# A hybrid decoder block: feature projections by seven products instead of eight, with weight parts streamed from DRAM

## The chip, the cores and the metric

One core of one Trainium2 chip runs the whole program. The metric is the device time in microseconds, the median of three runs. TensorE does the matrix products, VectorE (DVE), ScalarE (ACT) and GpSimd (POOL) the rest; SyncE (SP) issues transfers.

## What is computed

`x` has 4096 positions of 1024 features in f32. The layer is

```python
h = RMSNorm(x)
q, k, v, gk_lr, gate_g, u_p, gate_p, q_m, gate_m = split(h @ w_in)
gk = log_sigmoid(gk_lr @ w_gk_up + b_gk) / 16
o_gla = RMSNorm(gated_linear_attention(q, k, v, gk)) * silu(gate_g)  # 4 heads, chunks of 64
o_pool = (causal means of u_p - u_p) @ pool_w * pool_scale * silu(gate_p)
o_mem  = softmax(q_m @ k_m^T / 8) @ v_m * silu(gate_m)  # k_m, v_m from RMSNorm(mem)
y = RMSNorm(x + concat(o_gla, o_pool, o_mem) @ w_out)
```

`w_in` has 2576 columns: q and k 256 each, v 512, a low rank part of 16, gates 512 + 256 + 256, u_p 256 and q_m 256.

## The kernel before, in words

The sequence goes in 16 blocks of 256 positions. `run_blocks` writes block 0 (`first`), block 1 (`second`), a loop over blocks 2 to 14, block 15 (`last`) and a tail; every engine has its own list of instructions, ordered by hand, and semaphores between them.

**Precision.** A factor of a product stands in SBUF as two f16 parts, high and low, each weight group scaled by a power of two; a product is three matmuls (high x high, high x low, low x high) added up in PSUM. That is `split` (L371 to 378).

**Projections.** The block of x, transposed, 8 tiles of 128 features by 256 positions, is normalised in place (`normalise`, L1052) and split into `xn`: ACT makes the high parts (L725), GpSimd the low ones (L1416, two instructions of 1024 columns). The weights' parts are in `whl`, resident. `features` (L380) makes 256 output features of a block in one bank: 2 column halves x 8 tiles x 3 = 48 matmuls of 256 columns. A loop block has eight such groups (q, k, four of gates, u, qm), and the values in two halves (`split` with x as the weights, 24 matmuls of 512 columns each). The order on TensorE: low rank part (L425), q, logits of the decay (L440), k, a sum over partitions for the scale of the mixed block (`mix_sum`, L402), values, first two gates, u, qm, last two gates. ACT or DVE read each bank once: q and k on DVE with the decays (L1169 to L1179), the others on ACT (L843 values, L854 gates with silu, L869 u, L878 qm).

**Attention and output.** Then come the transposes of the keys (L512), the scores in chunks (L522), memory scores (L539), states, transposes of the softmax's probabilities (L563), the attention's products (L571, L577, L647) and the sums of squares of the heads (L585). The four quarters of the output projection of the block before (`out_proj`, L388, 24 matmuls of 512 columns each) stand between these steps. They need the mixed block's two parts: ACT's high part (`mixed_hi`, L787, after the values' first copy) and DVE's low part (`mixed_lo`, L1076 to L1093, whose first four small steps make the scale from bank 6). ACT turns the key transposes over (L902), after which it loads a table (L905) for the exponentials; output rows are squared and normalised on ACT (`norm_y`, L793 to L798). ACT's copy of the low rank part is L804.

**Preparation.** In block 0 each weight group gets a total (sums of squares on ACT, a matmul `total` on TensorE), a scale (`weights_scale`, DVE), high parts (`weights_hi`, ACT L733, ten pieces of 2048 columns) and low parts (`weights_lo`, DVE L1031, ten too); the memory's keys and values are multiplied out in f32 (L343, L348). W_out is read twice from DRAM in 8 tiles: squares in block 0, parts (`out_hi` L774, `out_lo` L1034) in block 1, resident in `wo`.

**Queues.** SP issues all transfers in one order: inputs, the next x block, W_out's tiles, and per block twice a residual in and, once its row is normalised (L1104 adds the residual), a store.

## Time and profile before

| | us |
|---|---|
| median of 3 runs | 1498.22 (1496.93 to 1498.28) |
| the profiled execution | 1497.08 |
| its span | 1495.6 |
| mean granted TensorE clock | 0.988 |
| busy: TensorE, VectorE, ACT, GpSimd | 1436.3, 709.6, 637.4, 215.1 |
| bytes moved by DMA | 73.70 MB |

The span runs from the first to the last instruction. The low rank matmuls (L425) mark a block's start: 22.9 for block 0, 136.35 for block 1, 226.78 for block 2, and from there one every 87.8 us until 1368.39, block 15. In the trace's rows an operation shows its start, its length, engine, line, operation, output and input tiles, the matmul's weight shape (128*128) and its moving shape. Groups show busy us, mean ns of one, and idle time ahead with what ended it. Times are of one execution.

### The profile page before, as it was taken

The numbers are of one execution on the slowest core, as the hardware profiler recorded it, in microseconds if no ns is written. First come the engines' busy times: TensorE is split into PE (matmuls) and PEld (weight loads), VectorE is DVE, ScalarE is ACT, GpSimd is POOL, SyncE is SP. The second block draws the span as 40 slices with busy tenths as digits, with TensorE's granted clock in tenths as the row PEclk, the third lists the DMA queues.
The fourth block names the chain that finished last, engine by engine and source line by source line (L and its number), as shares of the span: only waits on it lengthen the run. The fifth ranks groups of instructions, "written<-read, shape, count | busy, mean of one in ns | idle before, by whom it ended". The sixth has DMA issues, their size and how long they took to land.

```text
span 1495.6 us, 28176 instructions
## 1 busy us (share of the span) xinstructions
PE 1436.3 (96%) x11766; PEld 1043.1 (70%) x11766; DVE 709.6 (47%) x1357; ACT 637.4 (43%) x1135; POOL 215.1 (14%) x204
## 2 busy tenths in 40 slices
PE   4958999999999999999999999999999999999996
PEld 3747767768676776867667686776768677676852
DVE  4565454371635436172543717255271635527152
ACT  6676353442525344252533425254342624434241
POOL 2021020211201021020112102011210201121000
PEclk9979999999999999999999999999999999999998
DMA  9321201020110102001010200101020010201001
GB/s 361 127 85 60 83 29 58 1 85 0 40 44 28 56 0 84 0 28 56 20 64 0 84 0 28 56 14 70 0 84 0 28 56 4 80 0 57 1 29 71
DMA packets 18560, 73.70 MB, mean 49 GB/s; under 512 B 2016, under 2 KB 4320, under 8 KB 15712
## 3 DMA queue, kind: packets, MB, share of 16 engines
q1 hardware_dynamic: 18096, 72.96, 13.2%
q8 instruction: 24, 0.39, 0.1%
q10 hardware_dynamic: 432, 0.28, 0.1%
q14 instruction: 8, 0.07, 0.0%
HBM read 56.46 MB, written 16.78 MB: 49 GB/s over the span
## 4 chain that ended last, share of the span: by engine, by line
PE 93%; ACT 2%; DVE 2%; DMA 1%; issue 1%; POOL 1%; DVEq 0%; ACTq 0%
PE bank L377 77%; PE bank L539 2%; PE bank L563 2%; PE bank L571 2%; PE bank L577 2%; PE bank L585 2%; PE bank L647 1%; PE bank L550 1%; PE bank L440 1%; PE bank L425 1%; ACT whl L733 1%; PE bank L522 1%; PE bank L324 1%; PE bank L343 0%; PE bank L348 0%
## 5 line engine op out<-in xcount | busy, mean ns | idle before, releaser
L377 PE MATMUL bank<-arena,whl 128*128 128x256 f16 x6144 | 684.2, 274 | 0.0
L377 PEld LDWEIGHTS bank<-arena,whl 128*128 128x128 f16 x6144 | 602.0, 98 | 80.8 <-issue 4.0
L377 PE MATMUL bank<-arena 128*128 128x512 f16 x1536 | 344.0, 381 | 6.4 <-DVE arena L1093 6.4
L377 PEld LDWEIGHTS bank<-arena 128*128 128x128 f16 x1536 | 147.7, 98 | 181.3 <-issue 15.4
L1228 DVE SCALAR_TENSOR_TENSOR arena<-arena 64x256 f32<-64x256 f32 x60 | 25.2, 420 | 306.1 <-POOL arena L1440 304.7
L377 PE MATMUL bank<-whl,arena 128*128 128x512 f16 x768 | 168.5, 379 | 0.0
L854 ACT ACTIVATE arena<-bank,sca 128x512 f32<-128x512 f32 x60 | 41.3, 688 | 242.1 <-PE bank L377 242.1
L377 PEld LDWEIGHTS bank<-whl,arena 128*128 128x128 f16 x768 | 75.3, 99 | 86.8
L1416 POOL TENSOR_TENSOR arena<-arena 128x1024 f16<-128x1024 f32 x32 | 76.1, 2398 | 310.5 <-ACT arena L725 310.5
L1433 POOL TENSOR_TENSOR arena<-arena 128x542 f32<-128x542 f32 x16 | 17.4, 1090 | 657.4 <-ACT arena L869 657.4
L1267 DVE TENSOR_REDUCE mx<-bank 128x2 f32<-128x512 f32 x64 | 41.2, 684 | 141.6 <-PE bank L539 141.6
L1408 POOL TENSOR_TENSOR arena<-arena 128x1024 f32<-128x1024 f32 (+2 forms) x45 | 69.2, 1538 | 222.4 <-ACT arena L708 220.0
L1279 DVE SCALAR_TENSOR_TENSOR arena<-arena,rsum 128x256 f16<-128x256 f32 x128 | 61.6, 533 | 57.2 <-ACT arena L936 57.2
L1104 DVE SCALAR_TENSOR_TENSOR arena<-bank,sca,arena 128x512 f32<-128x512 f32 x64 | 47.8, 749 | 66.5 <-DMA arena<-in_x 42.4
L926 ACT ACTIVATE arena<-bank,nm,sca 128x256 f32<-128x256 f32 x128 | 71.2, 560 | 3.9 <-ACT nm L916 2.2
L936 ACT ACTIVATE arena<-arena,rsum 128x256 f16<-128x256 f32 x128 | 56.0, 499 | 25.6 <-DVE rsum L1273 25.6
L1093 DVE SCALAR_TENSOR_TENSOR arena<-arena,sca 128x2048 f16<-128x2048 f32 x16 | 37.6, 2352 | 49.8 <-ACT arena L787 49.8
L843 ACT ACTIVATE arena<-bank,sca 128x512 f32<-128x512 f32 x32 | 21.8, 685 | 88.6 <-PE bank L377 88.6
L793 ACT ACTIVATE arena<-arena 128x1024 bf16<-128x1024 f32 x32 | 33.6, 1050 | 55.6 <-DVE arena L1104 55.6
L1307 DVE COPY arena<-bank 128x1024 f16<-128x1024 f16 x64 | 43.9, 688 | 17.9 <-PE bank L563 17.9
L1052 DVE SCALAR_TENSOR_TENSOR arena<-arena,sca 128x256 f32<-128x256 f32 x128 | 51.9, 477 | 0.0
L878 ACT ACTIVATE arena<-bank 64x512 f16<-64x512 f32 x32 | 18.9, 592 | 69.8 <-PE bank L377 69.3
(164 smaller groups left out, 1441.1 us busy)
## 6 DMA issues: line engine op xcount, KB each, us to landing
arena<-in_xt SPq DMA_DIRECT2D x16, 1024.0 KB, 5.1
arena<-in_x SPq DMA_DIRECT2D x32, 512.0 KB, 3.3
out<-arena SPq DMA_DIRECT2D x32, 512.0 KB, 2.6
stage<-in_w_out SPq DMA_DIRECT2D x16, 512.0 KB, 4.8
arena<-in_w_v SPq DMA_DIRECT2D x1, 2048.0 KB, 14.6
whl<-in_w_mem SPq DMA_DIRECT2D x1, 2048.0 KB, 16.8
arena<-in_w_g SPq DMA_DIRECT2D x1, 2048.0 KB, 17.0
arena<-in_w_p SPq DMA_DIRECT2D x1, 2048.0 KB, 7.8
```

Of the source, the lines that this page charges most:

```text
L377: mm = nc.tensor.matmul(ap, lhs, rhs, start=k == 0 and n == 0, stop=(k, n) == last)
L854: nc.scalar.activation(gate[:, g:g + 2, :], bank[b][:, :].rearrange("p (a t) -> p a t", a=2), ACT.Silu, scale=sc_in[:, w:w + 1]).then_inc( ...
L926: a = nc.scalar.activation(pr[n % 2][:, h, :], bank[2 + n % 2][:, h * 256:(h + 1) * 256], ACT.Exp, bias=nm[:, 2 * n + h:2 * n + h + 1], sc ...
L936: a = nc.scalar.activation(phl[n % 2][:, 0, h, :], pr[n % 2][:, h, :], ACT.Copy, scale=rsum[:, 2 * n + h:2 * n + h + 1])
L1052: a = nc.vector.scalar_tensor_tensor(xb[:, k, :], xb[:, k, :], gx[:, k:k + 1], sq[:, 1, :], ALU.mult, ALU.mult)
L1093: nc.vector.scalar_tensor_tensor(mhl[:, 1, :, :], mixed, s_m, mhl[:, 0, :, :], ALU.mult, ALU.subtract).then_inc(m_lo, 1)
L1104: nc.vector.scalar_tensor_tensor(yb[:, c], bank[h][:, :], sc_out, yb[:, c], ALU.mult, ALU.add).then_inc(y_add, 1)
L1267: nc.vector.tensor_reduce(mx[:, 2 * n:2 * n + 2], bank[2 + n % 2][:, :].rearrange("p (h m) -> p h m", h=2), AX.X, ALU.max).then_inc(max_ok, 1)
L1279: a = nc.vector.scalar_tensor_tensor(phl[n % 2][:, 1, h, :], pr[n % 2][:, h, :], rsum[:, 2 * n + h:2 * n + h + 1], phl[n % 2][:, 0, h, :], ...
L1307: nc.vector.tensor_copy((pt0 if first else pt)[:, p, :, t * P:(t + 1) * P], b16[b].rearrange("p (a b) -> p a b", b=P)).then_inc(pt_out, 1)
L1408: nc.gpsimd.tensor_tensor(sq[:, 0:half, :], sq[:, 0:half, :], sq[:, half:2 * half, :], ALU.add).then_inc(sq_add, 1)
L1416: nc.gpsimd.tensor_tensor(xn[:, 1, k, :], xb[:, k, :], xn[:, 0, k, :], ALU.subtract).then_inc(x_lo, 1)
```

## The change

Two blocks of 256 features are projected together, by Strassen's scheme in Winograd's form. With two halves of the output features, two of the input features and two of the positions, the 8 block products become 7. The groups are QK (q and k), UM (u and qm), GG (the gates of the linear attention) and PM (pool and memory gates). A product is 2 x 4 x 3 = 24 matmuls of 128 columns. The 7 of a group come in three phases of 3, 3 and 1 (`PHASES`), into two banks that each hold two regions; between phases ACT copies regions to SBUF (`early_copies`, `second_copy`, `third_copy`) and the next phase goes on accumulating in the same regions; DVE adds copy and region for each quarter of the result (`add_11`, `add_12`, `add_2`). Phases of two groups alternate.

The x side needs four more inputs, B11-B12, B12+B22, that minus B11, and B21 minus that (`SG3`, `SG1`, `SG2`, `SG4`): GpSimd makes them and all low parts, ACT the high parts. The weight side needs four combinations too, made once in block 0 (on DVE for QK, on GpSimd for the others), so each group has 7 pieces of 1024 columns, each with a high and a low part. QK's, UM's and the values' parts are resident. GG's and PM's parts are written to DRAM in block 0 and W_out's in block 1; from then on each block reads 7 + 7 + 8 chunks of 512 KB into a ring of 8 slots.

The values' product (same size) moves behind all groups. Silu works on SBUF, in two pieces of 1024 columns. The attention steps stay.

```diff
+GG_SLOT = (0, 1, 2, 3, 4, 5, 6)
+PM_SLOT = (7, 0, 1, 2, 3, 4, 5)
+WO_SLOT = ((7, 0, 1, 2), (6, 3, 4, 5))
+B11, B12, B21, B22, SG1, SG2, SG3, SG4 = range(8)
+X_READY = {B11: 1, B12: 1, B21: 2, B22: 2, SG3: 3, SG1: 4, SG2: 5, SG4: 6}
+XPARTS = 6
+PHASES = (((0, B11, "a"), (1, B21, "c"), (2, SG3, "b")),
+          ((3, SG2, "a"), (4, B22, "b"), (5, SG4, "d")),
+          ((6, SG1, "a"),))
+REGION = {"a": (0, 0), "c": (0, 256), "b": (1, 0), "d": (1, 256)}
+BANKS = {QK: (0, 1), GG: (2, 3), UM: (4, 5), PM: (6, 7)}
+LANE = {QK: 0, GG: 1, UM: 0, PM: 1}
 STAGES = 3
...
+                sp.wait_ge(pe_f[GG], 3 * i + 1)
+                sides_in((1, 2, 3))
...
+                residual(i - 1, 0)
+                sp.wait_ge(pe_f[GG], 3 * i + 3)
+                out_in(((1, 0),))
+                sp.wait_ge(pe_f[PM], 3 * i + 1)
+                out_in(((0, 0), (0, 1), (0, 2)))
+                sp.wait_ge(pe_f[PM], 3 * i + 2)
+                out_in(((0, 3), (1, 1), (1, 2)))
+                sp.wait_ge(pe_f[PM], 3 * i + 3)
+                out_in(((1, 3),))
+                store(i - 1, 0)
+                residual(i - 1, 1)
+                if not last:
+                    sp.wait_ge(pe_out, 4 * i - 1)
+                    gates_in((0, 1, 2))
+                    sides_in((0,))
+                    sp.wait_ge(pe_out, 4 * i)
+                    gates_in((3, 4, 5, 6))
+                store(i - 1, 1)
...
+            def product(i, g, c, b, name, first):
+                if first:
+                    pe.wait_ge(lo_c, LATER[g] + c + 1)
+                elif g == GG:
+                    s = GG_SLOT[c]
+                    pe.wait_ge(d_slot[s], 16 * (3 * (i - 1) + 1) if s < 6 else 16 * (2 * (i - 1) + 1))
+                elif g == PM:
+                    s = PM_SLOT[c]
+                    pe.wait_ge(d_slot[s], 16 * (3 * (i - 1) + 2) if s < 6 else 16 * (2 * (i - 1) + 1))
+                if g == QK:
+                    pe.wait_ge(x_hi, XPARTS * i + X_READY[b])
+                    pe.wait_ge(x_lo, XPARTS * i + X_READY[b])
+                w, fresh = parts[g][c], c in (0, 2)
                 for j in range(2):
-                    c = c0 + j * P
-                    mm = split(bank[b][:, j * TB:(j + 1) * TB], KT,
-                               lambda k, p, r: (whl[:, p, k, c:c + P], xn[:, r, k, :]))
+                    ap = region(g, name)[:, j * P:(j + 1) * P]
+                    for k in range(4):
+                        for n, (p, r) in enumerate(((0, 0), (0, 1), (1, 0))):
+                            mm = nc.tensor.matmul(ap, w[:, p, k, j * P:(j + 1) * P], x_part(r, b)[:, k, :],
+                                                  start=fresh and j == 0 and k == 0 and n == 0, stop=k == 3 and n == 2,
+                                                  skip_group_check=True)
                 return mm
+            def phase(i, g, n, first):
+                if n == 1:
+                    pe.wait_ge(ad[g], 4 * i + 1)
+                    pe.wait_ge(cp[g], 4 * i + 2)
+                if n == 2:
+                    pe.wait_ge(cp[g], 4 * i + 3)
+                for c, b, name in PHASES[n]:
+                    mm = product(i, g, c, b, name, first)
+                mm.then_inc(pe_f[g], 1)
...
+                phase(i, QK, 0, first)
...
                 if first:
+                    fold_pool()
+                    phase(i, QK, 1, first)
+                    pe.wait_ge(mem_sum, 3)
+                    memory()
+                    phase(i, QK, 2, first)
+                    pe.wait_ge(w_scaled, 2)
+                    total(UM)
+                    pe.wait_ge(fold_out, 4)
+                    pe.wait_ge(w_scaled, 3)
+                    memory_kv()
+                    pe.wait_ge(mem_rs, 1)
+                    total(GG)
+                    pe.wait_ge(z_ok, 2)
+                    phase(i, UM, 0, first)
+                    pe.wait_ge(tops, 3)
+                    nc.tensor.matmul(all_vk, ones[:, :], kvmax[:, 0:2], start=True, stop=True).then_inc(w_tot, 1)
+                    pe.wait_ge(w_scaled, 4)
+                    pe.wait_ge(kv_scaled, 1)
+                    phase(i, GG, 0, first)
+                    phase(i, UM, 1, first)
+                    phase(i, GG, 1, first)
+                    phase(i, UM, 2, first)
+                    phase(i, GG, 2, first)
+                    pe.wait_ge(ad[UM], 4)
+                    total(PM)
+                    pe.wait_ge(lo_wv, 2)
+                    pe.wait_ge(ad[QK], 4)
+                    values(0).then_inc(pe_v, 1)
+                    pe.wait_ge(lo_vk, 1)
+                    pe.wait_ge(lo_vk, 5)
+                    phase(i, PM, 0, first)
+                    values(1).then_inc(pe_v, 1)
+                    phase(i, PM, 1, first)
                 else:
                     pe.wait_ge(mix_m, i)
+                    phase(i, GG, 0, first)
+                    phase(i, QK, 1, first)
+                    pe.wait_ge(o_st, 4 * i - 1)
                     mix_sum(i - 1)
...
+                    phase(i, GG, 1, first)
+                    phase(i, QK, 2, first)
+                    phase(i, GG, 2, first)
                     pe.wait_ge(z_ok, 2 * (i + 1))
...
+                    phase(i, UM, 0, first)
+                    pe.wait_ge(m_st, 4 * i - 3)
+                    if second:
+                        pe.wait_ge(o_scaled, 1)
+                    phase(i, PM, 0, first)
+                    phase(i, UM, 1, first)
+                    phase(i, PM, 1, first)
+                    phase(i, UM, 2, first)
+                    phase(i, PM, 2, first)
+                    pe.wait_ge(ad[GG], 4 * (i + 1))
+                    if not late(first, second) and not last:
+                        rms_sum(i + 1)
+                    pe.wait_ge(ad[QK], 4 * (i + 1))
+                    values(0).then_inc(pe_v, 1)
+                    values(1).then_inc(pe_v, 1)
                 pe.wait_ge(ke_ok, i + 1)
                 pe.wait_ge(kd_ok, i + 1)
                 pe.wait_ge(q_ok, 2 * (i + 1))
+                pe.wait_ge(ad[UM], 4 * (i + 1))
...
+            def early_copies(i, g):
+                act.wait_ge(pe_f[g], 3 * i + 1)
+                nc.scalar.activation(tp[LANE[g]][0], region3(g, "a"), ACT.Copy, scale=scale[g][0]).then_inc(cp[g], 1)
+                nc.scalar.activation(tp[LANE[g]][1], region3(g, "b"), ACT.Copy, scale=scale[g][1]).then_inc(cp[g], 1)
+            def second_copy(i, g):
+                act.wait_ge(pe_f[g], 3 * i + 2)
+                nc.scalar.activation(tp[LANE[g]][2], region3(g, "a"), ACT.Copy, scale=scale[g][0]).then_inc(cp[g], 1)
+            def third_copy(i, g):
+                act.wait_ge(pe_f[g], 3 * i + 3)
+                nc.scalar.activation(tp[LANE[g]][0], region3(g, "a"), ACT.Copy, scale=scale[g][1]).then_inc(cp[g], 1)
...
+                    second_copy(i, QK)
+                    if second:
+                        out_hi(2)
+                        out_hi(3)
+                    second_copy(i, GG)
+                    third_copy(i, QK)
+                    third_copy(i, GG)
+                    if second:
+                        out_hi(4)
+                        out_hi(5)
+                    else:
                         mixed_hi(i - 1)
+                    act.wait_ge(ad[QK], 4 * (i + 1))
+                    early_copies(i, UM)
+                    if not late(first, second) and not last:
+                        act.wait_ge(m_lo, i)
+                        squares(i + 1)
+                    act.wait_ge(ad[GG], 4 * (i + 1))
+                    early_copies(i, PM)
+                    if second:
+                        out_hi(6)
+                        out_hi(7)
+                        mixed_hi(i - 1)
+                    second_copy(i, UM)
+                    second_copy(i, PM)
+                    third_copy(i, UM)
+                    third_copy(i, PM)
+                    qm_split()
+                    if not late(first, second) and not last:
+                        rstd(i + 1)
+                    silu(0, GG)
+                    silu(1, PM)
+                    v_copy(0)
+                    v_copy(1)
+                nc.scalar.preload_act_table_set(EXP_LN)
...
+            def add_11(i, g):
+                dve.wait_ge(cp[g], 4 * i + 1)
+                nc.vector.scalar_tensor_tensor(cut(c_out[g][0], 0), region3(g, "c"), scale[g][0], tp[LANE[g]][0],
+                                               ALU.mult, ALU.add).then_inc(ad[g], 1)
+            def add_12(i, g):
+                dve.wait_ge(cp[g], 4 * i + 3)
+                nc.vector.scalar_tensor_tensor(cut(c_out[g][0], 1), region3(g, "b"), scale[g][0], tp[LANE[g]][2],
+                                               ALU.mult, ALU.add).then_inc(ad[g], 1)
+            def add_2(i, g):
+                dve.wait_ge(cp[g], 4 * i + 4)
+                nc.vector.scalar_tensor_tensor(cut(c_out[g][1], 1), region3(g, "a"), scale[g][1], tp[LANE[g]][1],
+                                               ALU.mult, ALU.add).then_inc(ad[g], 1)
+                nc.vector.scalar_tensor_tensor(cut(c_out[g][1], 0), region3(g, "d"), scale[g][1], tp[LANE[g]][0],
...
+                else:
+                    add_11(i, GG)
+                    if second:
+                        out_lo(0)
+                        out_lo(1)
+                    add_12(i, QK)
+                    add_12(i, GG)
+                    if second:
+                        out_lo(2)
+                        out_lo(3)
+                    dve.wait_ge(pe_msq, 2 * i)
+                add_2(i, QK)
...
+                else:
+                    add_2(i, GG)
+                    mixed_scale(i - 1)
+                    if second:
+                        out_lo(4)
+                        out_lo(5)
+                    else:
+                        mixed_lo(i - 1)
+                    dve.wait_ge(halo_ok, i + 1)
+                    add_11(i, UM)
+                    add_11(i, PM)
+                    if second:
+                        out_lo(6)
+                        out_lo(7)
+                        mixed_lo(i - 1)
+                    add_12(i, UM)
+                    add_12(i, PM)
+                    add_2(i, UM)
+                    add_2(i, PM)
```

TensorE, projections of a loop block before, from the second gates to u, qm and the next gates (`whl` is the weights; a wait names what ACT or DVE have done):

```order
L377 MATMUL bank<-arena,whl 128x256 [waits z_ok]
L377 MATMUL bank<-arena,whl 128x256 x47
L489 ISA
L377 MATMUL bank<-arena,whl 128x256 [waits v_out]
L377 MATMUL bank<-arena,whl 128x256 x47
L491 REGISTER_ALU
L377 MATMUL bank<-arena,whl 128x256 [waits v_out]
L377 MATMUL bank<-arena,whl 128x256 x47
L493 REGISTER_ALU
L377 MATMUL bank<-arena,whl 128x256 [waits gate_out]
```

and in the changed kernel the first phase of UM, PM's first and UM's second (`wres` resident parts, `ring` streamed ones, `cp_um` ACT's copies and `ad_um` DVE's additions of UM, `m_st` the steps of the mixed block's scale):

```order
L525 MATMUL bank<-arena,wres 128x128 [waits z_ok]
L525 MATMUL bank<-arena,wres 128x128 x71
L651 REGISTER_ALU
L525 MATMUL bank<-arena,ring 128x128 [waits d_slot7,m_st]
L525 MATMUL bank<-arena,ring 128x128 x23
L516 ISA
L525 MATMUL bank<-arena,ring 128x128 [waits d_slot0]
L525 MATMUL bank<-arena,ring 128x128 x23
L525 MATMUL bank<-arena,ring 128x128 [waits d_slot1]
L525 MATMUL bank<-arena,ring 128x128 x23
L525 MATMUL bank<-arena,wres 128x128 [waits cp_um,ad_um]
L525 MATMUL bank<-arena,wres 128x128 x71
```

A wait for the reader of another group has become a wait for copies and an addition of the same group.

DVE in a loop block before, from q's product with the decays to the mixed block's low part:

```order
L1169 SCALAR_TENSOR_TENSOR arena<-bank,sca,arena 64x2x256 [waits pe_o,pe_q,eb_ok]
L1169 SCALAR_TENSOR_TENSOR arena<-bank,sca,arena 64x2x256
L1171 COPY dec<-arena 128x8
L1177 SCALAR_TENSOR_TENSOR arena<-bank,sca,arena 128x512 [waits pe_msq,pe_k,enb_ok]
L1179 SCALAR_TENSOR_TENSOR arena<-bank,sca,arena 128x512 [waits ebl_ok]
L1079 TENSOR_SCALAR sca<-bank 128x1 [waits m_all]
L1081 TENSOR_SCALAR sca<-sca 128x1 [waits m_tiny]
L1084 TENSOR_SCALAR sca<-sca 128x1 [waits m_exp]
L1086 TENSOR_SCALAR sca<-sca 128x1
L1089 TENSOR_SCALAR sca<-sca 128x1 [waits m_inv]
L1093 SCALAR_TENSOR_TENSOR arena<-arena,sca 128x2048 [waits m_hi]
```

and in the changed kernel, from the products with the decays to UM's first addition (L1272):

```order
L1457 COPY dec<-arena 128x8
L1459 TENSOR_TENSOR arena<-arena 128x512 [waits ex_ok]
L1461 TENSOR_TENSOR arena<-arena 128x512 [waits ex_ok]
L1284 SCALAR_TENSOR_TENSOR arena<-bank,sca,arena 128x2x128 [waits cp_gg]
L1286 SCALAR_TENSOR_TENSOR arena<-bank,sca,arena 128x2x128
L1347 TENSOR_SCALAR sca<-bank 128x1 [waits m_all]
L1349 TENSOR_SCALAR sca<-sca 128x1 [waits m_st]
L1352 TENSOR_SCALAR sca<-sca 128x1 [waits m_st]
L1354 TENSOR_SCALAR sca<-sca 128x1
L1357 TENSOR_SCALAR sca<-sca 128x1 [waits m_st]
L1364 SCALAR_TENSOR_TENSOR arena<-arena,sca 128x2048 [waits m_hi]
L1272 SCALAR_TENSOR_TENSOR arena<-bank,sca,arena 128x2x128 [waits cp_um,halo_ok]
```

GG's additions (L1284, L1286) and then UM's (L1272) stand in one file with the decays, the scale (L1347 to L1357) and the low part (L1364).

ACT before, from the last gates to the first maximum, and then in the changed kernel:

```order
L854 ACTIVATE arena<-bank,sca 128x512 [waits pe_g]
L902 ACTIVATE arena<-bank 128x512 [waits pe_ket]
L905 ACT_TABLE_LOAD
L707 ISA [waits m_lo]
L708 ACTIVATE arena<-arena 128x2048 [waits d_x]
L916 ACTIVATE nm<-mx,sca 128x2 [waits max_ok]
```

```order
L1030 ACT_TABLE_LOAD
L1030 ACTIVATE arena<-arena 128x1024 [waits ad_gg]
L1030 ACTIVATE arena<-arena 128x1024 [waits ad_pm]
L1042 REGISTER_ALU
L1045 ACTIVATE arena<-bank,sca 128x512 [waits pe_v]
L1042 REGISTER_ALU
L1045 ACTIVATE arena<-bank,sca 128x512 [waits pe_v]
L1116 ACT_TABLE_LOAD
L1122 ACTIVATE arena<-bank 128x512 [waits pe_ket]
```

The values' copies (L1045) now stand directly ahead of the table load and the turned keys (L1122); the squares of the next block (L708 before) have moved ahead of these rows, to L854.

## Rows read from the trace of the kernel before

**Rows 1.** The page: span, busy time and instructions by engine, GB/s in 40 slices

```profile
span 1495.6 us, 28176 instructions
...
PE 1436.3 (96%) x11766; PEld 1043.1 (70%) x11766; DVE 709.6 (47%) x1357; ACT 637.4 (43%) x1135; POOL 215.1 (14%) x204
...
GB/s 361 127 85 60 83 29 58 1 85 0 40 44 28 56 0 84 0 28 56 20 64 0 84 0 28 56 14 70 0 84 0 28 56 4 80 0 57 1 29 71
```

**Rows 2.** Windows by stage: block 0, block 1, block 7

```profile
22.90:136.35 113.45, 90.66 (x744) 73.65 (x744) 65.84 (x132) 79.26 (x105) 13.51 (x13) 0.92 0.34 127
136.35:226.78 90.43, 90.43 (x729) 65.09 (x730) 49.85 (x91) 40.77 (x69) 14.13 (x14) 0.97 0.17 59
665.86:753.68 87.82, 87.82 (x731) 63.75 (x730) 40.94 (x78) 35.64 (x68) 13.44 (x12) 1.00 0.10 36
```

**Rows 3.** TensorE's timeline, end of block 7 and start of block 8

```profile
746.67 5.35 PE L377 MATMUL bank<-arena 128*128 128x512 f16 x24
...
754.23 5.42 PE L377 MATMUL bank<-arena,whl 128*128 128x256 f16 x48
759.48 1.03 PE L440 MATMUL bank<-arena,up 128*128 128x256 f32 x4
...
765.73 10.52 PE L377 MATMUL bank<-whl,arena 128*128 128x512 f16 x48
```

**Rows 4.** TensorE's timeline, sixteen transposes in block 7

```profile
734.12 1.06 PE L563 MATMUL bank<-ident,arena 128*128 128x128 f16 x16
735.02 5.34 PE L377 MATMUL bank<-arena 128*128 128x512 f16 x24
```

**Rows 5.** Groups of TensorE's weight loads by shape, whole program

```profile
L563 PEld LDWEIGHTS bank<-ident,arena 128*128 128x128 f16 x512 | 31.3, 98 | 6.0
```

**Rows 6.** ACT's timeline, start of block 8

```profile
755.42 1.04 ACT L793 ACTIVATE arena<-arena 128x1024 bf16<-128x1024 f32 x1
...
757.40 0.47 ACT L804 ACTIVATE arena<-bank,sca 128x256 f32<-128x256 f32 x1 [0.29 <-DVE arena L1315]
```

**Rows 7.** Groups of VectorE by shape, block 7

```profile
L1052 DVE SCALAR_TENSOR_TENSOR arena<-arena,sca 128x256 f32<-128x256 f32 x8 | 3.2, 476 | 0.0
...
L1093 DVE SCALAR_TENSOR_TENSOR arena<-arena,sca 128x2048 f16<-128x2048 f32 x1 | 2.4, 2352 | 3.4 <-ACT arena L787 3.4
...
L1313 DVE TENSOR_TENSOR arena<-arena 128x512 f32<-128x512 f32 x2 | 1.4, 686 | 1.5 <-ACT arena L978 1.5
...
L1079 DVE TENSOR_SCALAR sca<-bank 128x1 f32<-128x1 f32 x1 | 0.1, 150 | 0.0
```

**Rows 8.** Groups of ACT by shape, block 7

```profile
L787 ACT ACTIVATE arena<-arena,sca 128x2048 f16<-128x2048 f32 x1 | 2.0, 1992 | 0.0
...
L843 ACT ACTIVATE arena<-bank,sca 128x512 f32<-128x512 f32 x2 | 1.4, 688 | 6.3 <-PE bank L377 6.3
...
L905 ACT ACT_TABLE_LOAD x1 | 1.3, 1283 | 0.0
...
L902 ACT ACTIVATE arena<-bank 128x512 f32<-128x512 f32 x1 | 0.6, 589 | 0.0
```

**Rows 9.** Groups of GpSimd by shape, block 7

```profile
L1416 POOL TENSOR_TENSOR arena<-arena 128x1024 f16<-128x1024 f32 x2 | 4.7, 2357 | 18.9 <-ACT arena L725 18.9
```

**Rows 10.** Groups by shape, first 136 us, VectorE and ACT

```profile
L1031 DVE SCALAR_TENSOR_TENSOR whl<-arena,sca,whl 128x2048 f16<-128x2048 f32 x10 | 23.2, 2348 | 5.6 <-ACT whl L733 5.6
L733 ACT ACTIVATE whl<-arena,sca 128x2048 f16<-128x2048 f32 x10 | 19.6, 1994 | 9.5 <-DVE sca L1023 9.5
```

**Rows 11.** TensorE's timeline, block 0

```profile
53.91 7.15 PE L343 MATMUL bank<-whl 128*128 128x256 f32 x32
60.90 7.07 PE L348 MATMUL bank<-whl 128*128 128x256 f32 x32
...
96.13 1.89 PE L539 MATMUL bank<-kst,arena 128*128 128x256 f16 x8 [12.83 <-DVE arena L1244]
```

**Rows 12.** The page's DMA issues: count, KB each, us to landing

```profile
stage<-in_w_out SPq DMA_DIRECT2D x16, 512.0 KB, 4.8
```

1066 lines of the change are left out of this document (595 added, 471 removed).

## The prediction

> **What bounds the kernel now.** I read the page's busy times, then the windows by stage, then TensorE's timeline. The program's span is 1495.6 us and TensorE is busy for 1436.3 of it [rows 1]. The windows say where the rest is [rows 2]: block 0 (with the weights' preparation) takes 113.5 us and leaves TensorE free for 22.8; block 1 takes 90.4; a block of the loop takes 87.8 and TensorE is busy for all of it, at full granted clock, with ACT at 35.6 and DVE at 40.9. So in the loop time falls only if TensorE has less to do, and every new wait of TensorE is paid in full. The profiled execution took 1497.1 us (span plus 1.5); the median is 1.1 above. Less than 0.2% (3 us) can't be told from no change.
>
> **Term 1, the products, -4.5 us a block.** A group of 48 matmuls of 256 columns starts at 754.23 and what follows it at 759.48: 5.25 us, 109.4 ns each [rows 3]. Eight such groups are 42.0 us. The change issues 28 products of 24 matmuls, 672 of only 128 columns. What one of these costs is the open price. The nearest row is the same form: 16 f16 transposes of 128 columns, each with its own 128x128 load, from 734.12 to 735.02, 56 ns each [rows 4]. At 56 ns the 672 cost 37.6 us, 4.4 to 4.5 below 42.0. The other end: a load takes 98 ns by its own row, and there is one for every matmul [rows 5]; if loads could not overlap each other, 672 x 98 = 65.9 us. I take 56, because in rows 4 sixteen loads keep that pace as well. Values (48 of 512 columns, 10.4 us [rows 3]) and the output projection don't change in size.
>
> The Trainium skill, "TensorE: Matmul & The Clock Gate", section "Back-to-back issue gap", speaks against me: it gives about 81 ns sustained for a load and matmul at 128 columns, and 56 only for the isolated gap. By it Term 1 would be +12.4 us a block. The trace's 16 pairs don't agree with it, but they are a short burst after long matmuls; hence the rival below.
>
> **Term 2, new waits in a loop block, +4.4 us.** Before, a group had one reader copy in another bank and TensorE never asked for it soon. Now it returns to a bank of the same group after one other phase of 4.0 us (72 x 56 ns). Counted from the end of the attention's last product:
>
> *Logits.* ACT comes to the copy of the low rank part after the squares of the output rows: squares at 755.42, copy from 757.40 to 757.87 [rows 6], which is 11.2 us after the attention's end at 746.67 [rows 3]. The change puts two part copies of 512 columns ahead of it (0.6 each, by the 512-column copy [rows 8]): done at 12.4. TensorE has 7.6 us of other work after that end (746.67 to 754.23 [rows 3]) and then the first phase, 4.0 where a group was 5.25: ready at 11.6. Stall 0.9 with the hand-over.
>
> *Second phase of u and qm.* It wants DVE's first addition for that group. Ahead of that on DVE and ACT, from the end of the third phase of q and k: ACT's copy 0.5, two additions 1.0 (0.48 each by the 256-column row [rows 7]), four products with the decays and a small copy 3.0 (0.69 each [rows 7]), two additions 1.0, the scale of the mixed block 0.6 (four steps of 0.15 [rows 7]), ACT's high part 2.0 [rows 8], DVE's low part 2.35 [rows 7], the addition 0.5, and 0.5 of hand-overs: 11.5 us. TensorE meanwhile has a phase of 1.3 and two of 4.0: 9.4. Stall 2.1, of which 0.7 shows one phase earlier, where the first step of the scale must have read bank 6. Before, values and six groups covered all this.
>
> *Values last.* ACT copies the second half of the values (0.69), loads the table (1.28) and copies the turned keys (0.59) [rows 8] after the values end: 2.8 us with the hand-over. TensorE has transposes, scores and the first memory scores, 2.0 us. Stall 0.8. Before, the values' copies came five groups earlier.
>
> Four restarts at 0.15 are 0.6. Sum 4.4. GpSimd (1.2 us per 512 columns, half of 2.36 [rows 9]) has the parts of x ready: six steps after the attention's end, 12 us, wanted at 17. I cost it at nothing; if it were 5 us late, so would be TensorE.
>
> **Term 3, DRAM streams, 0 in the loop.** 22 parts of 512 KB a block, 11.5 MB, beside 3.1. In the program's first slice the page shows 361 GB/s [rows 1]; at that rate they need 32 of 88 us. A transfer of 512 KB lands in 4.8 us [rows 12]. Each is issued at the end of the phase that frees its slot and wanted 13 us later or more. On SP they stand behind stores that wait for the normalised rows; the closest case, the four last gate parts, is issued at 5 and wanted at 21.
>
> So a loop block is 87.8 - 4.5 + 4.4 = 87.7, bounds 84.5 (one stall in four stays) to 91 (they double). Thirteen blocks: -2 us.
>
> **Term 4, block 0, +31.** Weights go from 10 pieces of 2048 to 28 of 1024 and 2 of 2048: ACT 20 -> 33 us, DVE 23 -> 38 [rows 10], and 12 combinations of 1024 on GpSimd, 28 us [rows 9], each in line with DVE's low parts. What counts is the order, worked through from release to release with the prices of rows 7 to 11 taken by columns (no row is a release of the new order, so each time may be off by some us, the sum by 12):
> - First product at 25.5 (now 23.9). The total for the values' weights now stands before the logits and waits for ACT until 37; the last phase of q and k ends at 51.
> - The memory's keys and values wait for a scale that DVE makes after two additions, 3.0 of decays, 3.3 of memory norm, 4.7 of low parts and 1.0 of scale: 65, where they start at 53.9 today [rows 11]. Their two rows of 7.1 us [rows 11] end at 79.
> - DVE then has scale, two maxima, three low parts, an addition and the key scales: gates begin at 88.4, and five phases (14.7) end at 103.
> - ACT's squares of the last group (4.2) end at 108, TensorE's total waits for them in line. Half the values 5.2, then the last group part by part behind ACT, DVE and GpSimd: 130.4.
> - Additions, windows and low parts of q: memory scores at 136.9, where they now start at 96.1 [rows 11] with 21 us of gate groups still to come. These 21 us were the cover of the softmax. Without them its chain (maxima 1.4, exponentials 3.5, high and low parts 3.5, three squares of W_out 4.0, again 3.5 and 3.0, turns, copies 1.3, normalising x 3.3, then GpSimd's two sums 2.4 and two low parts 4.7) is bare: 167.5 for the start of block 1, which today is 136.35.
>
> **Term 5, block 1, +12.** ACT makes the last two squares of W_out before the logits (+4). W_out's parts go out to DRAM through two buffers and three stages; the third and fourth high part stand on ACT ahead of the copy that the gates' third phase needs, and the fourth waits for a write issued only after the gates' second phase, behind three parts: about 9 us idle. The next pair costs 3, the late parts of x 1.5; less what the loop's own stalls would have been (4). No row shows that write; bounds 0 and 20 (four round trips of 4.8 [rows 12]).
>
> The last block and the tail stay, within 1 us. **Sum: 1497.1 - 2 + 31 + 12 = 1538**, and since the median stands 1.1 higher, 1538 to 1539. I say 1538.
>
> **Rivals.**
> - *The waits are mostly covered.* If TensorE waits only 1 us a block (the additions slip in early, as DVE takes them while it would otherwise stand), the 13 loop blocks give 13 x 3.4 = 44: 1494; with block 0 at +20 it is 1483. It decides for faster when the stalls stay below 1.2 us a block, since 43 / 13 = 3.3. For it: DVE and ACT are idle for half of the block [rows 2]. Against: the chain of 11.5 us is single file, idle time elsewhere doesn't shorten it. Chance 0.17.
> - *The waits double*: each step of the single files costs a third more than its row (part views of PSUM and SBUF instead of whole ones), or GpSimd is late with the parts of x. 13 x 4.4 = 57: 1595, slower. Chance 0.15.
> - *The weight load is the bound.* At the 98 ns of rows 5, 65.9 us a block, 28.3 more than at 56, of which the stalls take back some 4: 16 x 24 = 390, 1930. Beside it, by the page's 81 ns, an estimate from that page: 16.8 more a block, some 1740. Decides from 63 ns on, where the products save nothing. Chance 0.08.
> - *The streams are late*, transfers landing one after another at 4.8 us: 22 x 4.8 = 106 us a block, 18 over: 1538 + 15 x 18 = 1810. Against: at the start transfers overlap. Chance 0.03.
> - Forecast, 1538: 0.57.
>
> **How the numbers follow.** The range starts at 1490, inside the first rival, and ends at 1592, just under the second's time: that leaves out a part of the faster case (0.06), half of the second (0.06), and the last two. Faster by over 0.2%: the first rival with the forecast's lower edge left out, 0.17. Same: 0.05. Slower: 0.78.
>
> **What would show it.** Matmuls of 128 columns at 56 ns start to start in TensorE's timeline; a loop block near 87.7 with four stalls, the largest (1 to 2 us) ahead of the second phase of u and qm, released by DVE; ones before the logits and before the first quarter of the output projection, released by ACT; no wait released by a DMA in the loop; block 1 starting at 160 to 175; in block 1 a wait of 5 to 10 us before the gates' third phase. I am wrong if a loop block is under 86 or over 90, or block 1 starts before 150.

## The result, and the profile after

The changed kernel takes **1623.4 us** (median of 4 runs, 1616.6 to 1628.2) where the kernel before, run beside it, takes 1497.8: ratio 1.084, 95% interval 1.081 to 1.087. Slower was forecast, but 1538 with a range up to 1592; the measured time lies 31 us above it.

The page after, its first lines, the clock in 40 slices and the queue of instruction transfers (they answer to [rows 1]; that queue had 24 packets and 0.39 MB before):

```profile
span 1621.0 us, 39404 instructions
...
PE 1423.9 (88%) x16380; PEld 1083.9 (67%) x16380; DVE 847.6 (52%) x1628; ACT 775.0 (48%) x1432; POOL 404.6 (25%) x344
...
PEclk9798889999999999899999999998999999999998
...
q8 instruction: 153, 2.51, 0.6%
```

TensorE is busy 12 us less than before and the span is 125 us longer, so all of it is time in which TensorE stands, or that it works at a lower clock. The windows by stage (block 0, block 1, block 6; as [rows 2]). A row holds the stretch and its length, then the busy us and, in brackets, the instructions of TensorE, of its weight loads, of DVE, ACT and GpSimd, and last the granted clock, the busy share of the DMA engines and GB/s:

```profile
25.10:179.70 154.60, 102.47 (x1037) 85.38 (x1037) 105.11 (x166) 99.39 (x142) 61.85 (x33) 0.81 0.41 152
179.70:284.86 105.16, 88.36 (x1019) 67.53 (x1019) 58.70 (x108) 51.78 (x92) 23.59 (x22) 0.94 0.55 193
655.86:750.63 94.77, 87.91 (x1016) 67.28 (x1017) 47.28 (x96) 43.73 (x86) 22.79 (x20) 0.95 0.43 158
```

Block 1 starts at 179.7 (forecast 167.5), block 2 at 284.9 (forecast 269.8, the 226.8 of before and terms 4 and 5), and the blocks behind it take 91.1 to 95.0 each, mean 93.1 (forecast 87.7). Where a loop block loses it stands at its very start. TensorE's timeline there (start us, us, line, operation, tiles; idle time ahead in brackets):

```profile
655.86 0.62 PE L583 MATMUL bank<-arena,wlr 128*32 128x256 f16 x16 [1.98 <-issue]
656.42 2.69 PE L525 MATMUL bank<-arena,wres 128*128 128x128 f16 x25
661.63 5.20 PE L525 MATMUL bank<-arena,wres 128*128 128x128 f16 x47 [2.52 <-issue]
666.62 1.21 PE L603 MATMUL bank<-arena,up 128*128 128x256 f32 x4
667.66 4.18 PE L525 MATMUL bank<-arena,ring 128*128 128x128 f16 x72
671.68 4.18 PE L525 MATMUL bank<-arena,wres 128*128 128x128 f16 x72
...
692.00 4.19 PE L525 MATMUL bank<-arena,wres 128*128 128x128 f16 x72 [1.06 <-DVE arena L1272]
...
716.72 5.34 PE L504 MATMUL bank<-ring,arena 128*128 128x512 f16 x24 [0.93 <-ACT arena L1122]
```

Three readings. A phase of 72 matmuls takes 4.02 us start to start (667.66 to 671.68), 55.8 ns each: term 1 holds. The two stands in the middle are the forecast ones, 1.06 for u and qm and 0.93 behind the values. But TensorE also stands 1.98 us ahead of the block and 2.52 us within the first phase, released by "issue", which is nothing that the profile shows, and the 47 matmuls behind the second stand take 5.0 us, twice their time. The clock of that whole stretch, of the part of it from the 4th of the 72 matmuls into the second stand, and of the stretch behind it:

```profile
655.86:666.62 10.76, 8.24 (x89) 7.77 (x89) 4.77 (x5) 2.84 (x7) 2.35 (x2) 0.54 0.78 293
656.60:661.00 4.40, 2.51 (x25) 2.24 (x22) 4.07 (x3) 2.10 (x6) 2.00 (x2) 0.50 0.73 288
667.66:675.70 8.04, 8.04 (x145) 8.04 (x144) 4.42 (x8) 4.44 (x9) 0.00 (x0) 1.00 0.30 98
```

0.50 is the lower of TensorE's two levels (1.2 of 2.4 GHz). The clock fell at 656.6, ahead of the second stand, so behind the first alone. In the twelve rounds with a branch ahead of them (blocks 3 to 14) it fell within 1.2 us of the block's start in five, and during or just behind the second stand in seven. Over the whole execution, TensorE's waits by releaser (us in total, times, longest):

```profile
PE bank L525 <- issue: 38.9, 13, 5.2
PE bank L583 <- issue: 19.7, 10, 2.6
PE bank L525 <- DVE arena L1272: 14.9, 14, 1.1
PE bank L583 <- ACT arena L881: 14.2, 4, 7.0
PE bank L455 <- ACT wres L848: 13.4, 2, 8.4
PE bank L504 <- ACT arena L1122: 13.4, 15, 0.9
PE bank L455 <- ACT wv L848: 10.9, 1, 10.9
PE bank L525 <- ACT arena L950: 10.8, 2, 9.4
```

Before, one wait of TensorE of 3.7 us was put down to "issue"; the first two rows are new in this size, and no term of the prediction holds them. What the trace adds: the transfers of the instruction queue are 16 KB each; before, none falls between 301 and 1369 us, in the loop's rounds after its first one. Now nine or ten fall in each round, and from block 3 to block 14 one begins 2.8 to 3.3 us after the block's start, beside the second stand. A round of the loop had 728 loads, 728 matmuls and 24 other instructions on TensorE; it now has 1016, 1016 and 56.

### The profile page after: what moved, and what is told of

Same layout as the page of the kernel before. It is cut to its first block, busy times and chain, and to the rows that moved or that the text cites. A ratio compares the mean times of both kernels' runs of the same rounds, so it can differ in the third digit from the quotient of the medians.

```text
span 1621.0 us, 39404 instructions
## 1 busy us (share of the span) xinstructions
PE 1423.9 (88%) x16380; PEld 1083.9 (67%) x16380; DVE 847.6 (52%) x1628; ACT 775.0 (48%) x1432; POOL 404.6 (25%) x344
## 4 chain that ended last, share of the span: by engine, by line
PE 64%; issue 7%; ACT 6%; DVE 5%; POOL 1%; DMA 1%; DVEq 0%; ACTq 0%; POOLq 0%
PE bank L504 28%; PE bank L525 26%; ACT arena L974 2%; PE bank L732 2%; PE bank L740 1%; PE bank L746 1%; PE bank L754 1%; PE bank L795 1%; ACT L1116 1%; PE bank L603 1%; PE bank L719 1%; DVE arena L1456 1%; DVE arena L1286 1%; PE bank L708 1%; DVE arena L1459 1%
## 5 line engine op out<-in xcount | busy, mean ns | idle before, releaser
L525 PE MATMUL bank<-arena,wres 128*128 128x128 f16 x5376 | 344.6, 228 | 50.3 <-issue 33.7
L525 PEld LDWEIGHTS bank<-arena,wres 128*128 128x128 f16 x5376 | 328.6, 103 | 59.4 <-issue 38.6
L504 PE MATMUL bank<-ring,arena 128*128 128x512 f16 x1536 | 343.9, 381 | 19.8 <-ACT arena L1122 13.4
L525 PE MATMUL bank<-arena,ring 128*128 128x128 f16 x5376 | 321.5, 221 | 14.7 <-ACT arena L950 9.4
L525 PEld LDWEIGHTS bank<-arena,ring 128*128 128x128 f16 x5376 | 310.6, 99 | 20.0 <-ACT arena L950 9.9
L504 PEld LDWEIGHTS bank<-ring,arena 128*128 128x128 f16 x1536 | 146.6, 98 | 198.1 <-issue 30.5
L504 PE MATMUL bank<-wv,arena 128*128 128x512 f16 x768 | 169.9, 381 | 0.0
L504 PEld LDWEIGHTS bank<-wv,arena 128*128 128x128 f16 x768 | 75.4, 98 | 89.5 <-issue 1.8
L950 ACT ACTIVATE arena<-bank,sca 128x256 f32<-128x256 f32 x64 | 30.1, 472 | 157.5 <-PE bank L525 157.5
L1727 POOL TENSOR_TENSOR arena<-arena 128x512 f16<-128x512 f32 x64 | 84.5, 1331 | 59.2 <-ACT arena L881 59.2
L1578 DVE TENSOR_REDUCE mx<-bank 128x2 f32<-128x512 f32 x64 | 41.2, 684 | 74.8 <-PE bank L708 74.8
L944 ACT ACTIVATE arena<-bank,sca 128x256 f32<-128x256 f32 x64 | 29.8, 465 | 101.5 <-PE bank L525 101.5
```

The source lines that it names most:

```text
L504: mm = nc.tensor.matmul(ap, lhs, rhs, start=k == 0 and n == 0, stop=(k, n) == last)
L525: mm = nc.tensor.matmul(ap, w[:, p, k, j * P:(j + 1) * P], x_part(r, b)[:, k, :], start=fresh and j == 0 and k == 0 and n == 0, stop=k == ...
L1578: nc.vector.tensor_reduce(mx[:, 2 * n:2 * n + 2], bank[2 + n % 2][:, :].rearrange("p (h m) -> p h m", h=2), AX.X, ALU.max).then_inc(max_ok, 1)
L1727: nc.gpsimd.tensor_tensor(x_part(1, b), sg[(m - 3) % 2], x_part(0, b), ALU.subtract).then_inc(x_lo, 1)
```

## The experiments

**Theories.** A: the loop's body no longer fits where TensorE keeps its instructions, so each round loads them again, and behind the branch back they come late. B: the parts of x are late (the profile names ACT L881 as the releaser at some block starts). C: the DRAM streams disturb TensorE.

**1. The loop written out.** In `run_blocks`, for every engine:

```diff
-            with eng.Fori(2, NB - 1) as i:
+            for i in range(2, NB - 1):
```

> The changed kernel with its loop over blocks 2 to 14 written out, so that TensorE takes no branch. Theory A (code loading): a loop block has 2032 loads and matmuls on TensorE and 56 other instructions of its queue, where the kernel before had 1456 and 24; the trace shows ten 16 KB instruction transfers in every round of the loop now and none before, and at the block's start TensorE stands twice (2.3 and 2.8 us) for nothing that the profile shows, then runs its next 70 matmuls at half clock (3.7 us). Written out, the fetches run ahead: both stands and the slow stretch go, a block falls from 93.4 to about 85, the total to 1510 to 1525. Theory B (the parts of x are late: the chain shows ACT and GpSimd as releasers at the block's start): nothing changes, 1615 to 1630. Theory C (the DRAM streams disturb TensorE): nothing changes either.

Measured **1538.2** (1536.5 to 1541.0; ratio to before 1.028, 1.026 to 1.029), 85 us less. TensorE's timeline at a block's start, and the window from there to the logits, then of the block:

```profile
635.90 0.62 PE L583 MATMUL bank<-arena,wlr 128*32 128x256 f16 x16
636.46 4.19 PE L525 MATMUL bank<-arena,wres 128*128 128x128 f16 x72
640.79 1.13 PE L603 MATMUL bank<-arena,up 128*128 128x256 f32 x4
```

```profile
635.90:640.79 4.89, 4.75 (x89) 4.36 (x88) 4.05 (x5) 4.79 (x11) 2.35 (x2) 1.00 1.00 379
635.90:721.95 86.05, 84.19 (x1018) 63.82 (x1017) 46.82 (x94) 43.25 (x85) 22.80 (x20) 1.00 0.46 172
```

The same 89 matmuls take 4.89 us instead of 10.76, at full clock, and every block from 3 to 14 takes 86.04 to 86.06 us. The streams are all still there (the DMA engines are as busy as they get, share 1.00, in that very window), and so are the parts of x. B and C fall. The total is above the expected 1510 to 1525: a block is 86.0, not 85, and block 2 still takes 91.6, with a wait for ACT's low rank copy behind block 1.

**2. The loop kept, with a hint for the branch back.**

```diff
-            with eng.Fori(2, NB - 1) as i:
+            with nc.Fori(2, NB - 1, engines=[eng.engine], hint_back_edge=True) as i:
```

```profile
641.01 0.62 PE L583 MATMUL bank<-arena,wlr 128*32 128x256 f16 x16
641.57 4.19 PE L525 MATMUL bank<-arena,wres 128*128 128x128 f16 x72
646.38 1.12 PE L603 MATMUL bank<-arena,up 128*128 128x256 f32 x4 [0.62 <-ACT arena L991]
```

A wait of 0.62 us for ACT's low rank copy shows ahead of the logits (in two rounds it is one of 0.7 and 0.9 us within the first phase instead). So it is not the loading that costs, it is loading that starts only once the branch has been taken.

**3. The kernel before, in matmuls of 128 columns.** The only thing taken from the change is the number of instructions:

```diff
-                    mm = split(bank[b][:, j * TB:(j + 1) * TB], KT,
-                               lambda k, p, r: (whl[:, p, k, c:c + P], xn[:, r, k, :]))
+                    for t in range(NT):
+                        mm = split(bank[b][:, j * TB + t * P:j * TB + (t + 1) * P], KT,
+                                   lambda k, p, r: (whl[:, p, k, c:c + P], xn[:, r, k, t * P:(t + 1) * P]))
```

> The kernel before with each matmul of its eight feature groups split into two of 128 columns: 1112 pairs of load and matmul a block (2224 instructions of TensorE) for 728; same products, same order, no part of the change. Theory A (code loading): instruction transfers appear in every round, two stands and a slow stretch come at the block's start, 7 to 9 us a block beside 768 x 56 ns against 384 x 109.4 ns (+1.0): total 1590 to 1625. Theories B and C: only the +1.0 a block, 1510 to 1520.

Measured **1543.2** (two runs; ratio 1.031, 1.028 to 1.033). Eleven transfers a round, and a stand just behind the branch:

```profile
682.40 0.28 PE L426 MATMUL bank<-arena,wlr 128*32 128x256 f16 x1
684.50 0.62 PE L426 MATMUL bank<-arena,wlr 128*32 128x256 f16 x15 [1.81 <-issue]
685.05 5.53 PE L377 MATMUL bank<-arena,whl 128*128 128x128 f16 x96
```

The loop's first round, ahead of which no branch goes back, is 88.9 us (the split itself costs 1.1), the later ones 90.4 to 91.1, the last 92.7. The mechanism is shown without Strassen, without streams and without the parts of x. Its size was forecast wrong: 2 us a block, not 7 to 9, since here only one stand comes, of 1.2 to 1.9 us, and the clock falls behind it in one round of twelve only, the last (in the round shown, 96 matmuls start to start in 5.37 us, 55.9 ns each).

**4. The kernel before, written out**, as in 1: the control.

> The kernel before with its loop written out: a control. Theory A: its loop has 1480 instructions on TensorE, no instruction transfer falls in rounds 3 to 14, TensorE never stands at the branch, so nothing is won: 1496 to 1500. If branches as such cost time (any loop), it would fall by 13 times that cost.

Measured **1498.3**, ratio 1.0006 (0.9995 to 1.0016). The page counts 93 instruction packets instead of 24, and no stand comes with them. A branch alone costs nothing measurable, and loading straight on costs nothing.

**5. Where the loop's head lies.** The changed kernel, loop kept, TensorE's loop head put at the start of a 16 KB block:

```diff
-            with eng.Fori(2, NB - 1) as i:
+            with nc.Fori(2, NB - 1, engines=[eng.engine],
+                         head_slot={eng.engine: 0} if eng.engine == nc.tensor.engine else None) as i:
```

> The changed kernel with its loop, whose first TensorE instruction is put at the start of a 16 KB fetch block. Theory A (code loading): the fetch behind the branch back is still not ahead, so the stand at the block's start (2.3 us) stays; but a whole block of 256 instructions then follows, in whose time the next one arrives, so the second stand (2.8 us) and most of the half clock stretch go: a block near 89 to 90, total 1570 to 1590. If where the page boundary lies does not matter: 1615 to 1630.

Measured **1566.9** (two runs; ratio 1.046, 1.044 to 1.048), 56 us less than the changed kernel, by the placement alone; a block takes 87.7 to 89.7 in most rounds. One stand is left, ahead of the block, and in the round shown the first phase runs at 56 ns:

```profile
647.21 0.62 PE L584 MATMUL bank<-arena,wlr 128*32 128x256 f16 x16 [1.47 <-issue]
647.76 4.19 PE L526 MATMUL bank<-arena,wres 128*128 128x128 f16 x72
```

With 93.1 before this edit and 86.0 written out, about 5 of the 7 us a round are the second stand and most of the half clock, and 2 the first stand. One stand can still bring the clock down: it falls in three of the twelve rounds, behind stands of 2.02, 2.33 and 1.86 us, and not in nine others with stands of 1.47 to 2.58. So the length of the stand alone doesn't decide it, and what does is not shown.

**6. How much fits.** The kernel before with four, then with six of its eight groups in matmuls of 128 columns (the edit of 3 for q, k and the first gates; then for u and qm as well).

> The kernel before with four of its eight feature groups in matmuls of 128 columns: 920 pairs and 24 others, 1864 TensorE instructions a round. If the store holds 2048 of them (1480 fit, 2088 did not): no instruction transfers after the loop's first round, a block 87.8 + 0.5, total 1503 to 1508. If it holds fewer than 1864: transfers in each round and some 2 us more a block, 1525 to 1535.

> The same with six groups: 1016 pairs and 24 others, 2056 instructions. If the store holds 2048: instruction transfers in every round and a stand at the branch, a block 87.8 + 0.8 + 2, total 1530 to 1540. If it holds more: none, total 1507 to 1512.

Both came out the other way. With 1864 instructions: 1538.6 (one run, and above even the 1525 to 1535 of the other branch), ten transfers and a stand of 1.4 to 2.3 us in each round, blocks of 90.1 to 92.4. With 2056: 1511.0 (one run), nine to eleven transfers a round, and no stand at all; every block takes 88.64. So 1864 instructions are reloaded in every round and 1480 were not.

Where the stand comes can be read from the traces by counting TensorE's records in the order of its list, the loop's body counted once. Written out, the changed kernel has 33317 records and 130 transfers, one for 256. The stand behind the branch comes after record 4289 in the changed kernel (the second stand), 4545 in that of experiment 3 and 3777 in the one with 1864: each is 193 more than a multiple of 256. So all three stand at the same place within stretches of 256, which can only be taken for the border between two 16 KB blocks. From the loop's head to that border it is 89 instructions in the changed kernel, 5 in the other two, 133 with 2056 and, by its edit, 256 in run 5, and the last two do not stand there. That fits one cause, the next block comes in time only if enough instructions lie ahead of the border; it was tried by an edit in run 5 alone. Why the changed kernel also stands ahead of its head, and the kernels made from the one before don't, stays open. By the same count the body of 1864 touches nine such blocks and the one of 1480 seven, so what is kept for a loop ends at seven or eight.

**7 to 10. The terms of the prediction, one by one,** each as one move in the written-out kernel (1538.2), at places where TensorE stands in it.

*The turned keys ahead of the table load* (ACT): `preload_act_table_set` moves behind the copy L1122.

> The written-out kernel (1538.2) with ACT's copy of the turned keys ahead of the table load instead of behind it. The prediction's own term: the output projection waits 0.65 to 0.9 us in every block for that copy, behind a load of 1.28. If the wait is paid in full and the exponentials do not take the load over: 15 x 0.8 = 12 us less, 1524 to 1530. Rival: the load now stands ahead of the exponentials, whose chain to the transposes is tight, and as much comes back there: 1535 to 1540.

Measured **1524.9** (1524.2 to 1525.6): 13.3 us less, a block 85.22. There are as many table loads as before, and no new wait of TensorE in a loop block for what they delay.

*UM first*: ACT's early copies of UM and PM, and DVE's first addition of UM, move ahead of other work:

```diff
-                        mixed_hi(i - 1)
                     act.wait_ge(ad[QK], 4 * (i + 1))
                     early_copies(i, UM)
+                    if not second:
+                        mixed_hi(i - 1)
...
-                        mixed_lo(i - 1)
                     dve.wait_ge(halo_ok, i + 1)
                     add_11(i, UM)
+                    if not second:
+                        mixed_lo(i - 1)
                     add_11(i, PM)
```

> The written-out kernel with UM's first copies and its first addition ahead of the mixed block's high and low parts (ACT and DVE) in the blocks of the loop. The prediction's chain: the second phase of u and qm waits 1.06 us in every block for that addition, in one file behind the scale and the low part. Moved ahead, the wait goes: 13 x 1.2 = 16 us less, 1520 to 1526. Rival: the wait moves to the next phase (PM's copies now stand behind the high part): 1530 to 1540.

Measured **1522.0** (1521.1 to 1523.2): 16.2 us less, a block 84.81. The phases follow without a gap (`wres` UM, `ring` PM):

```profile
656.95 4.19 PE L525 MATMUL bank<-arena,ring 128*128 128x128 f16 x72
660.98 4.18 PE L525 MATMUL bank<-arena,wres 128*128 128x128 f16 x72
665.00 4.18 PE L525 MATMUL bank<-arena,ring 128*128 128x128 f16 x72
```

*Block 1.* In the written-out kernel the gates' third phase waits as forecast; with W_out's parts 2 to 7 behind the gates' copies on ACT and DVE, and the second part sent out one step earlier on SP, that wait is gone, and the output projection waits for its parts instead:

> The written-out kernel; in block 1 W_out's parts 2 to 7 stand behind the gates' copies on ACT and DVE, and SP sends the second part out before it waits for the gates' second phase. The prediction's term 5: 10.7 us in which TensorE waits for a gate copy behind a part that waits for a write to DRAM. Theory: the 10.7 us go, block 1 falls from 106 to 95 or 97, total 1526 to 1531. Rival: the writes only end later, and the output projection of block 0 waits for its parts: 1533 to 1540.

The written-out kernel, then the one with the new order:

```profile
216.71 2.74 PE L525 MATMUL bank<-arena,ring 128*128 128x128 f16 x24 [10.69 <-ACT arena L950]
```

```profile
205.85 1.50 PE L526 MATMUL bank<-arena,ring 128*128 128x128 f16 x24
...
243.97 6.38 PE L505 MATMUL bank<-ring,arena 128*128 128x512 f16 x21 [4.33 <-DMA ring<-out_parts]
```

Measured **1531.3** (1530.1 to 1532.2): 6.9 us less; block 1 falls from 106.1 to 98.2. Both sides were partly right: 10.7 go, 4.3 come back.

*The values' total later* in block 0 (TensorE and DVE).

> The written-out kernel; in block 0 the total for the values' weights stands behind q and k's second phase on TensorE (and its scale later on DVE). TensorE stands 10.8 us there for ACT's squares, ahead of the logits. If that stand is on the path: up to 8 us less, 1530 to 1534. If DVE's low parts of q and k (until 40.6, twice as long as forecast while GpSimd makes parts of x) bound the start of the second phase anyway: the total is won 1 or 2 us, 1536 to 1538.

Measured **1536.8** (1535.0 to 1538.0): 1.4 us less. The stand of 10.8 us moves on to the matmuls of the folded pool weights, which now wait 9.9 us for a copy that stands behind the same squares on ACT. It was that file that was late, not the total.

**11. All of it together**, with three more moves in block 0: DVE's products with the decays behind UM's fourth low part; the load of the last weight group ahead of the gates' parts on SP, its squares earlier on ACT; q's low parts for the memory ahead of the windows on DVE.

> The written-out kernel with the four moves of the runs before together (turned keys ahead of the table load, UM first, W_out's parts behind the gates' copies, the values' total later) and three more in block 0: DVE's products with the decays behind UM's fourth low part, so that the memory's keys and values start some 5 us earlier; the load of the last weight group ahead of the gates' parts on SP and its squares some 8 us earlier on ACT; q's low parts of the memory ahead of the windows on DVE. The four moves brought 13.3, 16.2, 6.9 and 1.4 us alone: together 1500 if they add up. The three more are worth 5, 4 and 2 by the stands that TensorE shows there: 1489, range 1485 to 1500. Rival: they share one file (ACT), and block 0 gives 3 at most: 1497.

Measured **1494.3** (median of 11 runs, 1488.6 to 1495.2), ratio to before **0.9967, interval 0.9955 to 0.9978**: faster than both kernels, by a third of a per cent. Its blocks 0, 1 and 6:

```profile
24.71:170.03 145.32, 98.80 (x1036) 83.56 (x1036) 112.51 (x166) 98.81 (x142) 63.19 (x33) 0.84 0.44 162
170.03:269.95 99.92, 89.75 (x1018) 67.14 (x1019) 58.76 (x107) 51.37 (x91) 24.47 (x22) 0.93 0.57 202
612.51:696.50 83.99, 83.84 (x1018) 63.90 (x1018) 46.90 (x94) 43.40 (x85) 22.79 (x20) 1.00 0.48 177
```

A block is 83.99 where the kernel before needs 87.82 [rows 2], and TensorE is busy for all of it. Block 2 is the exception, with 90.6 and a wait of 4.1 us for ACT's low rank copy. So blocks 2 to 14 together take 1098.8 us where they took 1141.6, 43 less, and the preparation (start of block 2 at 270.0 against 226.8) takes just these 43 back. What remains is from block 15 and the tail, 122.8 against 127.2. Block 0 gave 10 us, a little less than the 11 hoped for.

## Why the prediction was wrong

**The step that failed** is the sum of the loop block, "So a loop block is 87.8 - 4.5 + 4.4 = 87.7". It counts what 672 matmuls of 128 columns take, not that they are 288 more instruction pairs in a loop. Matmuls and loads per round went from 1456 to 2032; the trace of before had the sign in it, no instruction transfer in the rounds of the loop, which I did not read. What the runs put in its place: 93.1 with the loop as it is, 86.0 written out. That is 7.1 us a round, 85 us in all by experiment 1. The forecast missed the time by the same 85, but not by this alone: the preparation came out 15 too long (terms 4 and 5, 284.9 against 269.8) and blocks 2 to 14 with the tail, but for the branch, 17 shorter than its terms, and these two nearly cancel. The loop block also met the prediction's own sign of being wrong (over 90). None of the rivals named the cause: "the waits double" is nearest in time (1595), but written out the waits are below the forecast, and "the streams are late" had transfers as its cause, but others, and a price of 18 us a block. The Trainium skill states the rule, in "Runtime: NRT & Kernel Launch", section "Instruction fetch mechanics": TensorE's store takes 128 KiB, 2048 instructions, refilled in blocks of 16 KiB, and a taken branch whose target is not in the current window of two blocks waits for a transfer. The traces agree on the 16 KB, on 256 instructions a block and on the wait behind a branch. They don't agree on a window of two: the body of 1480 lies across seven blocks and had no transfer in twelve rounds. The eight blocks of the 128 KiB are not contradicted, since the body of 1864 touches nine.

**Term 1** was right: 55.8 ns forecast as 56, over 672 matmuls in every block. The rival with the weight load as the bound fell, and so did the 81 ns sustained that the Trainium skill gives in "TensorE: Matmul & The Clock Gate", section "Back-to-back issue gap".

**Term 2**, 4.4 us of waits, was too much by 1.7 (86.04 against 87.7). The stand behind the values is there (forecast 0.8, measured 0.65 to 0.93; 0.82 a block by the turned keys' experiment), the one for u and qm is half of the forecast (2.1, measured 1.06; with its restart 1.2 by the one with UM first), the logits' hardly exists (0.9; the product starts 0.3 us behind the phase). I had added up the steps of both files as if each waited for the one before, and ACT and DVE overlapped more. The rival "mostly covered" needed waits below 1.2 us a block; they are 86.0 - 83.3 = 2.7. The 0.15 for a restart had no row behind it: the wait of 1.06 brought 1.23 when it went, so a restart is about 0.17 there. The 0.5 for hand-overs has no row either, and no run measures it. Doubled waits would give 92.1 a block, where the prediction writes 91.

**Term 3**, the streams, was right: no wait of TensorE in the loop was released by a transfer of data.

**Term 4**, block 0, was too small by 12: block 1 starts at 179.7, not 167.5. The files were the right ones; two prices were not. DVE's low parts of 1024 columns were priced at half of 2.35 [rows 10]. While GpSimd makes parts of x they take 2.2 us, and 1.27 behind that (DVE's, then GpSimd's timeline of the changed kernel):

```profile
25.96 2.17 DVE L1251 SCALAR_TENSOR_TENSOR wres<-arena,sca,wres 128x1024 f16<-128x1024 f32 x1
...
36.67 2.17 DVE L1251 SCALAR_TENSOR_TENSOR wres<-wres,sca 128x1024 f16<-128x1024 f32 x1
38.76 1.27 DVE L1251 SCALAR_TENSOR_TENSOR wres<-arena,sca,wres 128x1024 f16<-128x1024 f32 x1
```

```profile
24.91 2.14 POOL L1727 TENSOR_TENSOR arena<-arena 128x512 f16<-128x512 f32 x1
...
33.53 4.23 POOL L1727 TENSOR_TENSOR arena<-arena 128x512 f16<-128x512 f32 x2
```

GpSimd's last operation ends at 37.8. Six operations of DVE lose some 0.9 each, 5 us in all. They reach TensorE by way of ACT, which waits for two of DVE's combinations:

```profile
32.54 1.15 ACT L892 ACTIVATE wres<-wres,sca 128x1024 f16<-128x1024 f32 x1 [2.61 <-DVE wres L1297]
...
36.84 1.15 ACT L892 ACTIVATE wres<-wres,sca 128x1024 f16<-128x1024 f32 x1 [1.59 <-DVE wres L1299]
```

So ACT's squares for the values' total end at 42.6 where I had 37, and q and k's second phase stands behind that total; DVE's own low parts are done at 41.2. The Trainium skill, "SBUF — State Buffer", section "SBUF: two separate sides", has this as a lock that either engine holds for a whole instruction, when DVE reads two operands from SBUF; the two rows fit, and no run took one engine away. The second price is the clock: 0.81 in block 0, so that the first f32 row of the memory takes 9.4 us in the written-out kernel where I had 7.1 [rows 11]. The two prices make some 7 of the 12. Against the forecast's times the changed kernel is 7 us late at the end of q and k (58 for 51), 10 at the end of the memory's keys and values (88.7 for 79) and 12 at the memory scores (148.6 for 136.9); the rest was not split up.

**Term 5**, block 1, had the right mechanism with 9 us forecast and 10.7 measured, and the squares ahead of the logits (4, measured 4.7). What it left out is the half clock behind these stands (a mean clock of 0.94 in block 1, and 72 matmuls in 4.7 us instead of 4.0). Block 1 took 105.2, forecast 102.4 (90.4 [rows 2] and 12); the term's own parts, 4, 9, 3 and 1.5 less 4, add up to 13.5.

Written out, the change takes 1538.2, the forecast to a tenth of a per cent. That is not the forecast come true: there block 2 starts at 286.1, 16 us later than forecast, and blocks 2 to 14 and the tail are 17 us shorter than its terms.

## What to carry to other kernels

Before making a loop body's matmuls smaller or more numerous, count TensorE's instructions in a round, and look for instruction transfers in the rounds of the trace: where there are none yet and the count grows by a quarter or more, price a stand at every branch back, a second one where a 16 KB border lies close behind the loop's head, and a clock that may fall behind either. The cure is cheap and can be tried before the rest is judged: write the loop out, or give the hint, or move the loop's head. And when a change trades a little of a bound engine for waits of others, test the waits one by one: four moves, each at a stand of TensorE, brought 38 us one by one where the written-out version was 41 behind, and with three more it came out ahead.
